# Each expert's weights in one transfer on one semaphore, issued once the slot's down product is done

## The reference

```python
grp_prob = softmax(x @ w_grp + b_grp)            # 4 groups, the best one is taken
e_logits = x @ w_rt + b_rt                       # 8 experts in the group, the best 2 are taken
comb = ...                                       # (640, 32): weight of each expert for each row
for gi in range(N_GROUPS):
    sl = slice(gi * E_PER_GROUP, (gi + 1) * E_PER_GROUP)
    hg = silu(einsum('nd,edf->nef', x, w_gate[sl])) * einsum('nd,edf->nef', x, w_up[sl])
    out = out + einsum('nef,efd->nd', hg * comb[:, sl, None], w_down[sl])
```

## Time and profile before

| What | us |
|---|---|
| Median of 3 runs | 1329.68 (1323.46 to 1339.95) |
| The profiled execution's own time | 1339.29 |
| Its span, first to last instruction | 1337.5 |
| Busy: PE / DVE / ACT / POOL | 1085.6 / 400.5 / 293.8 / 201.9 |
| Expert weights: gate/up half, issue to landing, median of 34 | 13.4 |
| Expert weights: down half, issue to landing, median of 34 | 12.9 |

### The profile page before, as it was taken

How to read it: one execution, slowest core, us unless ns; L and a number is a source line. 1 busy time by engine, 2 the same in 40 slices (tenths; PEclk the granted TensorE clock), 3 DMA queues, 4 the chain that set the end, 5 groups by cost and what they waited for, 6 DMA issues and landing times.

```text
span 1337.5 us, 15604 instructions
## 1 busy us (share of the span) xinstructions
PE 1085.6 (81%) x5706; PEld 647.7 (48%) x5706; DVE 400.5 (30%) x929; ACT 293.8 (22%) x596; POOL 201.9 (15%) x226
## 2 busy tenths in 40 slices
PE   7899999995767777999799998699727777777760
PEld 4454555444666666666344557344324334444430
DVE  1301323325464554434421004122561111111115
ACT  3001456534221222210200003012001222222211
POOL 1000555301010000100200000001402222222224
PEclk9899999996987868999899998899958999999995
DMA  9211103101311111500654300652129999999985
GB/s 341 66 63 63 63 1 142 64 0 68 119 71 64 63 63 63 158 0 0 211 189 147 126 1 1 251 200 115 79 94 372 423 424 423 424 424 424 425 329 237
DMA packets 65625, 227.09 MB, mean 170 GB/s; under 512 B 14768, under 2 KB 24112, under 8 KB 52528
## 3 DMA queue, kind: packets, MB, share of 16 engines
q1 hardware_dynamic: 57680, 200.14, 39.0%
q0 software_dynamic: 7760, 26.22, 4.9%
q10 hardware_dynamic: 144, 0.17, 0.0%
HBM read 205.11 MB, written 21.40 MB: 169 GB/s over the span
## 4 chain that ended last, share of the span: by engine, by line
PE 55%; DMA 18%; issue 16%; DVE 7%; ACT 2%; POOL 1%; SPq 0%; DVEq 0%; POOLq 0%; ACTq 0%
PE bank L417 16%; PE bank L413 16%; DMA sb_W<-w_experts 15%; PE bank L2122 5%; PE bank L1104 3%; PE bank L551 2%; PE bank L1644 1%; DMA sb_act_a<-h_rows,sb_attn 1%; PE bank L774 1%; PE bank L562 1%; DMA sb_W<-cache_mem 1%; PE bank L1617 1%; PE bank L1109 1%; PE bank L794 1%; PE bank L1708 1%
## 5 line engine op out<-in xcount | busy, mean ns | idle before, releaser
L413 PE MATMUL bank<-sb_act_a,sb_W 128*128 128x512 f32 (+1 forms) x768 | 213.0, 435 | 0.0
L417 PE MATMUL bank<-sb_W,sb_act_a 128*128 128x512 f32 x400 | 184.2, 608 | 1.7 <-issue 1.0
L2122 PE MATMUL bank<-sb_W,sb_act_b 128*64 128x256 f32 x1088 | 126.9, 386 | 48.0 <-DMA sb_W<-w_experts 47.0
L413 PEld LDWEIGHTS bank<-sb_act_a,sb_W 128*128 128x128 f32 x768 | 116.0, 191 | 91.2 <-issue 90.5
L2122 PEld LDWEIGHTS bank<-sb_W,sb_act_b 128*64 128x64 f32 x1088 | 83.3, 138 | 105.4 <-issue 42.4
L417 PEld LDWEIGHTS bank<-sb_W,sb_act_a 128*128 128x128 f32 x400 | 74.4, 194 | 87.3 <-issue 85.7
L1104 PE MATMUL bank<-sb_x 128*128 128x128 f32 x512 | 72.7, 295 | 13.2 <-DVE sb_x L1493 9.7
L2177 DVE TENSOR_TENSOR sb_act_b<-bank,sb_act_b 128x128 f32<-128x128 f32 x34 | 9.9, 291 | 239.5 <-ACT sb_act_b L2150 239.5
L2133 PE MATMUL bank<-sb_W,sb_act_b 128*64 128x512 f32 x272 | 65.9, 604 | 15.7 <-DVE sb_act_b L2179 15.7
L1104 PEld LDWEIGHTS bank<-sb_x 128*128 128x128 f32 x512 | 65.8, 205 | 19.8 <-DVE sb_x L1493 9.2
L2097 POOL DMA_INDIRECT pair_rows<-sb_act_b,sb_attn x34 | 33.6, 988 | 217.8 <-ACT sb_act_b L2154 217.8
(11 more groups left out here) (381 smaller groups left out, 1437.4 us busy)
## 6 DMA issues: line engine op xcount, KB each, us to landing
sb_W<-w_experts SPq DMA_DIRECT2D x34, 2048.0 KB, 13.4
sb_W<-w_experts SPq DMA_DIRECT2D x34, 1024.0 KB, 12.9
sb_W<-cache_diff SPq DMA_DIRECT2D x16, 1024.0 KB, 6.3
sb_W<-cache_mem SPq DMA_DIRECT2D x16, 1024.0 KB, 7.1
sb_W<-w_in SPq DMA_DIRECT2D x6, 2048.0 KB, 8.5
sb_W<-pair_rows POOLq DMA_DIRECT2D x10, 512.0 KB, 8.0
sb_x<-x_prompt SPq DMA_DIRECT2D x8, 512.0 KB, 6.8
sb_W<-w_out SPq DMA_DIRECT2D x2, 2048.0 KB, 8.2
```

Of the source, the lines that this page charges most:

```text
L413: mm = nc.tensor.matmul(out[:, 0:cols.stop - cols.start], slot(unit)[:, c, m * P:(m + 1) * P], src[:, c, cols], start=c == 0, stop=c == KC ...
L417: mm = nc.tensor.matmul(out[:, :], src[:, c, ja * P:(ja + 1) * P], w, start=c == 0, stop=c == KC - 1)
L2122: mm = nc.tensor.matmul(bank[2][64 * g:64 * g + 64, 0:256], xgT[k][:, c % 4, 64 * (c // 4):64 * (c // 4) + 64], w_gu(k)[:, c, g, :], start ...
```

## The change

Per block, SP issues one DMA of the expert's 3 MiB (24 KB a row) on one semaphore per slot, `s_e`. It goes out when the slot's down product is done. PE's gate/up product waits for that semaphore, and the down product no longer waits for weights.

```diff
-        s_eg = [sem(f"expert_gate_up_loaded{k}") for k in range(2)]
-        s_ed = [sem(f"expert_down_loaded{k}") for k in range(2)]
+        s_e = [sem(f"expert_loaded{k}") for k in range(2)]
...
                 src = a["w_experts"][bass.ds(e, 1)].rearrange("o p n -> (o p) n")
-                sp.wait_ge(e_pe["gu"], e_pe.after(j - 2, "gu"))
-                sp.dma_start(W[:, k, 0:4096], src[:, 0:4096]).then_inc(s_eg[k], 16)
                 sp.wait_ge(e_pe["d"], e_pe.after(j - 2, "d"))
-                sp.dma_start(W[:, k, 4096:6144], src[:, 4096:6144]).then_inc(s_ed[k], 16)
+                sp.dma_start(W[:, k, :], src).then_inc(s_e[k], 16)
...
                     pe.wait_ge(e_dve["h"], e_dve.after(j - 1, "h"))
-                    pe.wait_ge(s_eg[k], i * 16 + 16)
+                    pe.wait_ge(s_e[k], i * 16 + 16)
...
                     pe.wait_ge(e_dve["hT"], e_dve.after(j, "hT"))
-                    pe.wait_ge(s_ed[k], i * 16 + 16)
                     pe.wait_ge(e_act["y"], e_act.after(j - 1, "y"))
```

## The result

The change is slower. The median went from 1326.57 us (4 runs, 1321.37 to 1339.95) to 1384.24 us (4 runs, 1381.63 to 1389.94), a ratio of 1.0424 with a 95% interval of [1.0336, 1.0513]. The forecast was 1344 us, with a range to 1358. Runs of one kernel fall into a faster and a slower group, and each ratio compares the faster runs of both kernels, so that it is not the quotient of the medians beside it.

The account below looks back on a forecast made before the run. DMA engines bound the expert loop, 17.32 us a round. A later start plus 0.7 us a round over 15 rounds gave about +14 us: 1344 us from a 1329.68 median, range 1328 to 1358.

Parts of the forecast that it names:

- The start: Entry to the expert loop: expert 2's refill goes out at 1017.33, lands 10.6 us later, gate/up starts about 1028.0.
- The long rows: Weight DMA: one 24 KB row for two saves about 9 ns a row, 0.08 us per engine and expert.
- The fixed cost per DMA: Rival, weights' queue: each DMA costs a fixed time and the change saves one per expert; 1251 us, 3%.
- The gathers: Rival, expert loop: gathers land late, after 14.5 us, and hold up the transposes; round 19.5 us, 1367 us; 12%.
- no change in the products' 7.4 us: Slot's cycle: landing to refill issue stays at the 7.4 us read from the kernel before.
- The cycle that I forecast, 18.0 us: Expert loop: one slot's products, 7.4 us, plus refill, 10.6 us; 0.7 us over the present round.
- a falling clock: Expert loop: listed among the signs that the forecast is wrong, with no size and no chance.
- the refill, "taken 10.6": Slot's cycle: 3 MiB load from issue to landing, middle of 9.75 (nothing beside it) and 11.4 us (gathers beside it).
- the lower end of 9.75: Refill bound from the first expert's load, nothing beside it: 9.83 us less 0.08 for longer rows; 0 us change overall.

Follow-up runs that it names:

- the longer wait alone: Kernel before, its two weight DMAs issued as they were, but gate/up waits for both halves: 1333.45 us, ratio 0.9983.
- four products behind the down product: Changed kernel with four added constant products on TensorE after the odd slot's down product, into a bank nothing reads: 1365.18 us, ratio 1.0265.
- both halves late: Kernel before with its gate/up half issued after the down product, beside the down half; two DMAs, each with its own wait: 1334.59 us, ratio 0.9935.

## Why the prediction was wrong

**What held.** The mechanism in outline: a slot's cycle is products plus refill, SP's queue runs empty once a round, and the DMA engines no longer bound the loop. The start: expert 2's gate/up was put at about 1028.0 and came at 1028.35. The long rows: a 24 KB row took 912 ns in the median of the packet records, against 923 by the prediction's own rule of bytes and 9 ns. The fixed cost per DMA: nothing was saved (the section of the Trainium skill that the prediction cites for 2.0 us describes DMAs issued from GpSimd, and these loads are SP's). The gathers: TensorE's list of waits has no wait for one, although the scatters take 11.1 us to land for 8.2. The Trainium skill, DMA: Bandwidth & Descriptors, section "Queues, rings and completion order", has an engine alternate between queues; the packet records agree as far as they go, since they name no engine: 4 KiB packets keep starting among the 24 KB rows of a load in flight, and in the holes of the weights' queue.

**The step that failed: "no change in the products' 7.4 us".** I took the time from landing to refill issue from a kernel in which the clock stays at 1.00 and did not ask what the idle time would do to it. Before, TensorE waits 47.0 / 15 = 3.1 us a round, in two pieces of at most 1.9 us; the other 14.2 us of the round are products and short waits between them. The cycle that I forecast, 18.0 us, thus has 3.8 us of idle time in it. I never placed them. With both slots gated by their own refills, the slot whose refill comes out of an empty queue waits for the whole of it, the other's has landed by then, and all of the idle time lies ahead of one gate/up. Behind such a stretch that product took 5.3 to 6.3 us for 3.67 in 15 of the 16 rounds from expert 2 on, which by itself makes the slot's 7.4 us into the 9.8 of the chain. The rows of this case show that the stretch's length alone does not decide it: in the changed kernel 3.20 us ahead of expert 2 went with a gate/up of 5.36 us, and 3.52 us ahead of expert 4 with one of 3.67; with the longer wait alone, 1.96 us went with 5.36. The Trainium skill, TensorE: Matmul & The Clock Gate, section "HAM oscillation — how this bites in real kernels", describes a kernel in which each tile's products wait for a DMA and so each tile starts at the lower clock; the trace agrees for the even slot, with 0.59 granted in that product and 1.00 in the odd slot's. I had named a falling clock as what would make the forecast wrong, and gave it no rival, no price and no chance. By the run with four products behind the down product it is 17.6 of the 47.5 us, with the doubt about the split that stands there.

**The mis-sized term: the refill, "taken 10.6" between 9.75 and 11.4.** In the changed kernel the even refill takes 10.4 to 11.3 us, within the ends. But that is beside products that run slow. With the clock held by four products the refill that sets the round takes 10.8 to 12.3 us, mean 11.7, past the upper end in most rounds, and the round is 19.1 us, not 18.0. Two things stand in it that the first loads' rows could not show: up to 2.9 us of the other slot's rows still ahead of it in the queue, and 2.1 us of gathers and scatters beside it. The prediction had bounded their part by a load with gathers beside it and nothing ahead of it; taking most of their bytes away gave back about 1 us a round.

A restart of the queue is in it too, but it was not left out. In the packet records of the changed kernel the first 16 rows of an even load, one for each DMA engine, take 1.7 us in the median and up to 2.5, for 0.91 of the others; beside the median row that is 0.9 us per engine and round. But the first expert's load, behind the lower end of 9.75, begins with such rows as well (0.7 us per engine). In the kernel before, and with both halves late, no weight row of the loop was slow.

**The sum.** Of the +47.5 us of the profiles, 4.2 are the start (3.9 forecast). Of the 43.2 in the loop (9.9 forecast), 25.6 remain with the clock held and 17.6 go with the run of four products behind the down product. None of the clock's part was forecast. At 0.5 to 1.8 us a round over 15.5 rounds it lies between some 8 and 28 us, an estimate from the rounds with and without a fall.

**Open.** How the 43.2 us of the loop divide between the clock and the refill stays within the bounds above. What decides whether a given idle stretch brings the clock down was not found. That the slow product keeps the slots bunched is argued from the traces, that of the longer wait alone above all, and was not tested by itself.

## What to carry to other kernels

A double-buffered load that a queue serves without a hole has slack in its queue time; add up everything that a change takes from that slack, since edits that each cost nothing cost their excess together. Where a product will wait for a transfer, place the idle time, do not only sum it: here 4.1 us a round, mostly in one piece, brought TensorE's clock down in nearly every round, and 3.1 us in two pieces, in the kernel before, did not. A short stretch is no guarantee: one of 1.96 us brought it down too. And price the products behind such a wait at the lower clock as the forecast's bound, even where the profile before shows the clock at its full level.

## What the runs showed of the hardware

- TensorE's granted clock fell about once a round of 20 us, behind idle stretches of 2.6 to 4.4 us in the changed kernel, with products before and after. It stayed up behind one of 3.52 us, and fell behind one of 1.96 us in the run with the longer wait alone.
- A queue that has drained restarts slowly: 1.7 us in the median and up to 2.5 for the first 16 rows of 24 KB, 0.91 us for the others.
- Gathers and scatters of 256 KB beside 24 KB rows, with the clock held or nearly held, made a round of two loads about 1 us longer (19.14 against 17.94 us).
- A product of 128x128 by 128x512 in fp32 on constants, added in fives, took 0.88 us at a clock of 1.00, not the 0.49 us that I had reckoned.
